# A recurrent block that starts from unscaled activations, with its norm factor applied behind its products

## What is computed

```
def rms_norm(x, g):
    y = x * rsqrt(mean(x * x, axis=-1) + 1e-6)
    return y * g

def rglru_block(h, w_in, conv_w, conv_b, w_a, b_a, w_x, b_x, lam, w_o):
    proj = h @ w_in                                   # 256 x 2048
    gate = gelu(proj[..., :1024])
    xc = causal_depthwise_conv(proj[..., 1024:], conv_w, conv_b)     # 4 taps
    r = sigmoid(per-block(xc @ w_a) + b_a)            # 16 blocks of 64 x 64
    i = sigmoid(per-block(xc @ w_x) + b_x)
    log_a = -8 * r * softplus(-lam)
    a, mult = exp(log_a), sqrt(-expm1(2 * log_a))
    hs = scan over tokens of  h = a * h + mult * i * xc
    return (hs * gate) @ w_o

x = x + rglru_block(rms_norm(x, norm_mix[1]), ...)
x = x + squared_relu_mlp(rms_norm(x, norm_mlp[1]), ...)
```

## Time and profile before

| | us |
|---|---|
| median of 3 runs (lowest, highest) | 1701.01 (1700.12, 1701.41) |
| the profiled execution, its own time | 1701.29 |
| its span | 1699.4 |
| busy over the span: PE / DVE / ACT / POOL | 1414.4 / 1087.3 / 557.2 / 530.9 |
| granted clock of PE over the span | 0.926 |

### The profile page before, as it was taken

One profiled execution on the slowest core, in us unless ns is written; L12 is line 12 of the kernel. 1 busy time (PEld: TensorE's weight loads), 2 busy tenths in 40 slices (PEclk: granted clock), 3 DMA queues, 4 the chain that ended last, 5 costly groups with the idle time before them and its releaser, 6 DMA issues.

```text
span 1699.4 us, 25116 instructions
## 1 busy us (share of the span) xinstructions
PE 1414.4 (83%) x9312; PEld 1069.9 (63%) x9312; DVE 1087.3 (64%) x2131; ACT 557.2 (33%) x1037; POOL 530.9 (31%) x620
## 2 busy tenths in 40 slices
PE   8999999986999999999988937677777648676766
PEld 7889999976999999878888823232222213222222
DVE  5556774487677456987765975757576557457435
ACT  5554653347565343432151122111121211112111
POOL 8100000010000000000000575666666666666664
PEclk9999999998999999999999968988898879888888
DMA  7444655534465453322243897999999999999997
GB/s 232 133 133 125 189 184 170 191 113 130 143 189 182 151 191 105 113 64 77 76 155 118 328 405 296 380 359 370 370 340 359 364 364 377 371 369 359 357 377 293
DMA packets 206242, 407.91 MB, mean 240 GB/s; under 512 B 10626, under 2 KB 136876, under 8 KB 206140
## 3 DMA queue, kind: packets, MB, share of 16 engines
q0 software_dynamic: 74096, 269.52, 41.2%
q1 hardware_dynamic: 131884, 136.54, 25.2%
q10 hardware_dynamic: 160, 0.53, 0.1%
HBM read 405.49 MB, written 1.05 MB: 239 GB/s over the span
## 4 chain that ended last, share of the span: by engine, by line
PE 51%; issue 14%; another core or an unknown queue 12%; DVE 11%; POOL 7%; ACT 4%; DMA 1%; POOLq 0%; DVEq 0%; SPq 0%; ACTq 0%
PE banks L2114 12%; PE banks L2116 11%; PE banks L2115 11%; PE banks L2545 3%; PE banks L2304 3%; PE banks L2580 3%; POOL arena L872 2%; POOL wring L872 2%; DVE arena L1969 2%; PE banks L2401 1%; DVE h_raw L1604 1%; PE banks L2099 1%; POOL h_raw L872 1%; ACT arena L1302 1%
## 5 line engine op out<-in xcount | busy, mean ns | idle before, releaser
L1359 DVE TENSOR_TENSOR w_a_low<-wring,w_a_high 128x1024 fp32r<-128x1024 f32 x192 | 235.0, 1226 | 128.1 <-ACT w_a_high L913 126.2
L872 POOL DMA_INDIRECT arena<-in_expert_u_dram,eidx x99 | 92.9, 939 | 656.3 <-DVEq L1949 597.3
L913 ACT ACTIVATE w_a_high<-wring 128x1024 fp32r<-128x1024 f32 x192 | 201.6, 1052 | 147.2 <-PE banks L2116 145.3
L2114 PE MATMUL banks<-h_high,w_a_high 128*128 128x256 f32 (+1 forms) x832 | 238.0, 286 | 7.9 <-DVE h_low L1367 7.3
L1302 ACT ACTIVATE arena<-ident,arena 128x128 f32<-128x128 f32 x238 | 83.9, 395 | 478.9 <-remote 249.6
L2116 PE MATMUL banks<-h_high,w_a_low 128*128 128x256 f32 (+1 forms) x832 | 235.1, 283 | 0.0
L2115 PE MATMUL banks<-h_low,w_a_high 128*128 128x256 f32 (+1 forms) x832 | 235.1, 283 | 0.0
L2580 PE MATMUL banks<-arena 128*128 128x512 f32 x340 | 169.3, 645 | 74.2 <-ACT arena L1302 40.0
L2580 PE MATMUL banks<-wring,arena 128*128 128x512 f32 x308 | 159.5, 662 | 54.5 <-issue 22.0
L2580 PEld LDWEIGHTS banks<-arena 128*128 128x128 f32 x340 | 67.1, 205 | 176.4 <-issue 128.7
L2114 PEld LDWEIGHTS banks<-h_high,w_a_high 128*128 128x128 f32 x832 | 157.8, 190 | 9.7 <-issue 7.6
(11 more groups left out here) (413 smaller groups left out, 2767.9 us busy)
## 6 DMA issues: line engine op xcount, KB each, us to landing
wring<-in_mlp_w_dram SPq DMA_DIRECT2D x64, 1024.0 KB, 5.3
wring<-in_w_in_dram SPq DMA_DIRECT2D x19, 1024.0 KB, 5.4
wring<-in_sb_w_qkv_dram SPq DMA_DIRECT2D x12, 1024.0 KB, 5.1
wring<-in_rg_w_in_dram SPq DMA_DIRECT2D x8, 1024.0 KB, 5.9
wring<-in_w_q_dram SPq DMA_DIRECT2D x8, 1024.0 KB, 5.2
wring<-in_sb_w_o_dram SPq DMA_DIRECT2D x4, 1024.0 KB, 6.3
wring<-in_rg_w_o_dram SPq DMA_DIRECT2D x4, 1024.0 KB, 5.4
wring<-in_w_o_dram SPq DMA_DIRECT2D x4, 1024.0 KB, 7.7
```

The source lines that it names most:

```text
L872: g.indirect_dma_start(out=grow(j), out_offset=None, in_=(expert_u, expert_v)[which][0], in_offset=bass.IndirectOffsetOnAxis(ap=eidx[:, tt ...
L913: a.activation(unit(n, 0), raw_unit(n), ACT.Copy).then_inc(w_high, 1)
L1359: v.tensor_tensor(unit(n, 1), raw_unit(n), unit(n, 0).bitcast(F32), ALU.subtract).then_inc(w_split, 1)
L2114: mm(dst, left[0], right[0], start=first, stop=False)
```

## The change

- `last_input` now serves both layers: in `mlp(0)` too, ACT writes the high part of x * gain and the square of each part of `xT` (4 parts after 18 of the down projection's weight splits, 2 near the end, the last 2 as they come), and DVE the low parts. `norm(2)` is gone from ACT and DVE.
- PE starts `rg0` at once, makes the norm's sums behind it (bank `ms2`), and transposes the keys behind `rg15`.
- ACT makes `rs` from the bank by Ln and Exp, as in the attention layer: no reciprocal on DVE, no square root.
- DVE takes all 16 groups out of their banks, times `rs`: rg0 to rg7 into `xraw` ahead of the taps (ACT's copy is gone), rg8 to rg15 into `gate` (`gate_input`) in pieces between the steps of the block's end. ACT's gelu then reads `gate`.
- ACT's tanh follows the sigmoids group by group (`decays`); its exponentials for `aS` stand behind each half's root.
- DVE copies the keys behind the splits of `m_hl` and three weight splits, ahead of the residual.

```diff
@@ -181,15 +181,16 @@
...
-            plan.add("ms2")
-            for m in range(4):
-                plan.add(f"key{m}")
             for m in range(KT + 2):
                 plan.add(f"rg{m}", m - KT if m >= KT else None)
+                if m == 0:
+                    plan.add("ms2")
                 if m >= 2:
                     plan.add(f"ri{m - 2}", BANKS + KT - 1 - m if m >= KT else None)
             for m in range(KT + 2, 2 * KT):
                 plan.add(f"rg{m}", m - KT)
+            for m in range(4):
+                plan.add(f"key{m}")
             for m in range(KT):
                 plan.add(f"rgo{m}")
...
@@ -927,28 +929,27 @@
...
-                if layer == 0:
-                    split_high(MLP_UNITS - hidden - UNITS)
-                    return
-                act.wait_ge(meta_ready, 1)
-                a.activation(h_hl[0][:, :, 0:META], meta_g[:], ACT.Copy).then_inc(meta_high, 1)
-                a.activation(sq[:, :, 0:META], xT[:, :, 0:META], ACT.Square).then_inc(meta_high, 1)
+                if layer:
+                    act.wait_ge(meta_ready, 1)
+                    a.activation(h_hl[0][:, :, 0:META], meta_g[:], ACT.Copy).then_inc(meta_high, 1)
+                    a.activation(sq[:, :, 0:META], xT[:, :, 0:META], ACT.Square).then_inc(meta_high, 1)
                 split_high(18)
                 for kt in range(4):
-                    last_input(kt)
+                    last_input(layer, kt)
...
                 split_high(3)
                 for kt in range(6, 8):
-                    last_input(kt)
-                split_high(2)
...
+                    last_input(layer, kt)
+                split_high(1 + layer)
+
+            def last_input(layer, kt):
+
+                gain = g_both if layer else par[:, KT:2 * KT]
+                act.wait_ge(x_ready, KT * (2 + 2 * layer) + kt + 1)
                 a.activation(h_hl[0][:, kt, real], xT[:, kt, real], ACT.Copy,
-                             scale=g_both[:, kt:kt + 1]).then_inc(h_high, 1)
+                             scale=gain[:, kt:kt + 1]).then_inc(h_high, 1)
                 a.activation(sq[:, kt, real], xT[:, kt, real], ACT.Square).then_inc(sq_ready, 1)
...
@@ -1038,7 +1039,10 @@
...
-            norm(2, whole=2, after=UNITS)
+            pb = wait_group(act, "ms2")
+            link(a.activation(rtmp[:, 0:SEQ], pb[:, 0:SEQ], ACT.Ln, bias=eps[:, 3:4]))
+            act.sem_inc(free("ms2"), 1)
+            a.activation(rs[:, 0:SEQ], rtmp[:, 0:SEQ], ACT.Exp, scale=-0.5).then_inc(rs_ready, 1)
...
@@ -1048,23 +1052,24 @@
...
+            def decays(m):
+
+                sigmoids(m)
+                act.wait_ge(ri_ready, m + 1)
+                a.activation(tS[:, m, :], rS[:, m, :], ACT.Tanh, scale=lamc[:, 3, m:m + 1]).then_inc(at_ready, 1)
+
             act.wait_ge(xc_ready, 1)
+            act.wait_ge(lam_ready, 2)
             for m in range(KT):
-                pb = wait_group(act, f"rg{m}")
-                a.activation(xraw[:, m, CONV - 1:], pb[:, 0:SEQ], ACT.Copy).then_inc(free(f"rg{m}"), 1)
                 split_high()
                 if m >= 3:
-                    sigmoids(m - 3)
+                    decays(m - 3)
...
-            sigmoids(KT - 3)
-            sigmoids(KT - 2)
+            decays(KT - 3)
+            decays(KT - 2)
             split_high()
-            sigmoids(KT - 1)
-            act.wait_ge(ri_ready, KT)
-            act.wait_ge(lam_ready, 2)
-            for m in range(KT):
-                a.activation(tS[:, m, :], rS[:, m, :], ACT.Tanh, scale=lamc[:, 3, m:m + 1]).then_inc(at_ready, 1)
+            decays(KT - 1)
...
@@ -1072,23 +1077,23 @@
...
-            for m in range(KT):
-                a.activation(aS[:, m, :], rS[:, m, :], ACT.Exp, scale=lamc[:, 4, m:m + 1]).then_inc(at_ready, 1)
             for m, h4 in enumerate(halves):
                 act.wait_ge(m_ready, m + 1)
                 a.activation(mS[:, h4], mS[:, h4], ACT.Exp, scale=0.5).then_inc(mroot_ready, 1)
-                split_high()
+                for k in range(h4.start, h4.stop):
+                    a.activation(aS[:, k, :], rS[:, k, :], ACT.Exp, scale=lamc[:, 4, k:k + 1]).then_inc(at_ready, 1)
+            for m in range(KT):
+                act.wait_ge(gate_in, m + 1)
+                a.activation(gate[:, m, :], gate[:, m, :], ACT.Gelu_apprx_tanh).then_inc(gelu_done, 1)
             split_high()
-            for m in range(KT):
-                pb = wait_group(act, f"rg{KT + m}")
-                a.activation(gate[:, m, :], pb[:, 0:SEQ], ACT.Gelu_apprx_tanh).then_inc(free(f"rg{KT + m}"), 1)
             for m in range(2):
...
                 a.activation(m_hl[0][:, h4, :], gate[:, h4, :], ACT.Copy).then_inc(gate_high, 1)
+            split_high(2)
             norm(3, whole=1, units=True)
...
@@ -1485,12 +1490,12 @@
...
+                    if k == 18:
+                        last_input(layer, 0, 4)
                     if k < hidden - UNITS:
                         split_low()
-                    if layer and k == hidden - UNITS:
-                        last_input(4, 6)
+                    if k == hidden - UNITS:
+                        last_input(layer, 4, 6)
                         split_low(2)
...
@@ -1500,21 +1505,22 @@
...
-                    if layer and k >= hidden - 2:
-                        last_input(k - hidden + KT, k - hidden + KT + 1)
+                    if k >= hidden - 2:
+                        last_input(layer, k - hidden + KT, k - hidden + KT + 1)
...
-            split_low(UNITS)
+            split_low(2)
...
@@ -1522,14 +1528,21 @@
...
-            norm(2, 1)
-            for m in range(4):
...
+            dve.wait_ge(xc_ready, 1)
+            dve.wait_ge(rs_ready, RS_AT[2])
+
+            def gate_input(first, last_):
+
+                for k in range(first, last_):
+                    pb = wait_group(dve, f"rg{KT + k}")
+                    link(v.tensor_tensor(gate[:, k, :], pb[:, 0:SEQ], rs[:, 0:SEQ], ALU.mult))
+                    dve.sem_inc(free(f"rg{KT + k}"), 1)
+                    dve.sem_inc(gate_in, 1)
 
             for m in range(KT):
-                wait_out(dve, f"rg{m}")
+                pb = wait_group(dve, f"rg{m}")
+                link(v.tensor_tensor(xraw[:, m, CONV - 1:], pb[:, 0:SEQ], rs[:, 0:SEQ], ALU.mult))
+                dve.sem_inc(free(f"rg{m}"), 1)
...
@@ -1542,28 +1555,35 @@
...
+            gate_input(0, 3)
             halves = [slice(0, KT // 2), slice(KT // 2, KT)]
             for m, h4 in enumerate(halves):
                 dve.wait_ge(at_ready, KT + 2 * m + 2)
                 link(v.tensor_tensor(mS[:, h4], mS[:, h4], tS[:, h4], ALU.subtract))
                 dve.sem_inc(m_ready, 1)
+                gate_input(3 + m, 4 + m)
...
-            dve.wait_ge(at_ready, 2 * KT + 4)
...
                 link(v.tensor_tensor(iS[:, h4], iS[:, h4], mS[:, h4], ALU.mult))
+                gate_input(5 + m, 6 + 2 * m)
+                dve.wait_ge(at_ready, KT + 4 + 4 * (m + 1))
...
                 settle()
-                split_low(2 if m else 1)
             for m, h4 in enumerate(halves):
-                wait_out(dve, *[f"rg{KT + k}" for k in range(h4.start, h4.stop)])
+                dve.wait_ge(gelu_done, h4.stop)
                 v.tensor_tensor(gate[:, h4], gate[:, h4], rS[:, h4], ALU.mult).then_inc(y_ready, 1)
...
                                 ALU.subtract).then_inc(y_split, 1)
+            split_low(3)
+            for m in range(4):
+                pb = wait_group(dve, f"key{m}")
+                v.tensor_copy(keyT[:, 4 * m:4 * m + 4, :].rearrange("p a n -> p (a n)"),
+                              pb[:, :]).then_inc(free(f"key{m}"), 1)
             residual([f"rgo{m}" for m in range(KT)], mlp_norm=3)
...
@@ -2249,26 +2269,26 @@
...
-            norm(2)
+            def gate_inputs(m):
...
+
+            for m in range(2 * KT):
+                project([f"rg{m}"], "rg_in", h_real, ready=h_wait(2) if m == 0 else None, first=m)
+                if m == 0:
+                    norm(2)
+                if 2 <= m < KT + 2:
+                    gate_inputs(m - 2)
...
-            for m in range(2 * KT):
-                project([f"rg{m}"], "rg_in", h_real, ready=h_wait(2) if m == 0 else None, first=m)
-                if 2 <= m < KT + 2:
-                    gate_inputs(m - 2)
             project([f"rgo{m}" for m in range(KT)], "rg_o", m_all, ready=lambda kt: (y_split, kt // 4 + 1))
...
```

More of the change, by code:

```diff
@@ L1487, in mlp @@
                 for k in range(hidden):
-                    if layer and k == 18:
-                        last_input(0, 4)
+                    if k == 18:
+                        last_input(layer, 0, 4)
                     if k < hidden - UNITS:
                         split_low()
-                    if layer and k == hidden - UNITS:
-                        last_input(4, 6)
+                    if k == hidden - UNITS:
+                        last_input(layer, 4, 6)
                         split_low(2)
@@ L2251, in _ @@
```

(15 more changed lines are left out.)

21 lines of the change are left out of this document (9 added, 12 removed).

## The result

| | before | after |
|---|---|---|
| median of 11 runs each, same chip, us | 1701.2 | 1685.5 |
| lowest, highest | 1692.55, 1703.22 | 1678.99, 1692.2 |
| ratio, 95% interval | | 0.9913 (0.9897 to 0.9928) |
| the profiled execution, its span | 1701.29, 1699.4 | 1684.46, 1682.7 |
| busy PE / DVE / ACT / POOL | 1414.4 / 1087.3 / 557.2 / 530.9 | 1407.3 / 1087.8 / 556.7 / 531.7 |

The kernel is faster by 12 to 17.5 us (the interval of the ratio, times 1701.2). In the block itself PE's busy time hardly moved: 84.8 us of 106.5 before, from 344.40 to the last residual addition, and 84.2 of 93.2 after, so what went there is time in which PE stood. The 7 us that PE's busy time fell by over the span lie almost all behind the block, in the same 6084 instructions (997.1 us before, 990.1 after, 1000.5 in a second profile of after).

What follows compares the result with a forecast made beforehand. PE was taken as the bound, with standstills in the head and before the output projection. First output product at 410.5 instead of 426.0 takes 15.5 us off 1701.3: 1685.8, less 0.3 is 1685.5 us; range 1682.3 to 1690.

Steps and rivals of the forecast that it cites:

- Head: From down projection to norm factor: rg0 starts without waiting, sums end at 350.85 us, `rs` ready at 351.95.
- The down projection: Rival: ACT or DVE work of `last_input` delays weight splits and PE starves, up to 6.4 us, 1692; chance 0.05.
- Convolution: Loop behind the norm sums: DVE's round 3.72 us, PE's 3.70, slack shrinking from 2.2 to 2.0; PE stays the limit.
- The rival in which DVE becomes the limit: In the convolution, DVE's round is 4.2 us, not 3.72; PE loses 1.8 us, total 1689; chance 0.16.
- Bank 0: New PE wait at rg8 until ACT frees the bank after ri4's sigmoids: 1.1 us, bounds 0 to 2.
- Block weights: Loads needed by ri0 at 356.6 us, forecast to land between 352.6 and 357.7 us.
- the rival of 0 to 1.1 us: At ri0, PE waits that long for late weights, up to 1686.6 us; counted within the forecast's chance of 0.56.
- The flip to slower: At ri0, weights landing after 372.1 us cancel the gain, from 376 slower by over 0.2%; chance 0.02.
- Tail: From rg10's end at 387.3 us to first output product, 23.2 us on DVE's chain: 410.5 instead of 426.0.
- Keys: Transpositions on PE right behind rg15, taken as 1.9 us; no wait for their banks was forecast.
- Clock: PE's clock falls to 0.50 in a 6.9 us standstill before the output products, as before: nothing gained or lost.
- Behind the tail: Output projection to residual: DVE starts 2.4 us late but catches up by the eighth group; cost 0, at most 1.

Runs made afterwards that it cites:

- all three together: Changed kernel with ri4's sigmoids earlier, block weights issued before the memset, and no DVE waits for its own gate reads: median 1684.58 us, ratio 0.9903.
- weights early: Changed kernel with block weights issued ahead of GpSimd's memset, which then writes only zero blocks: first output product 0.82 us earlier, span 1690.6 us.
- weights late: Changed kernel with GpSimd's memset of the block weights' area made four times: first output product 3.0 us later, span 1697.0 us.
- Factor first: Changed kernel with norm sums first and PE waiting for the norm factor before rg0: first output product 0.64 us later, span 1687.4 us.
- old tail: Changed kernel with tanh after the last sigmoids, exponentials ahead of roots, gate inputs behind scans: first output product at 73.71 us, not 67.78; span 1692.7 us.

## Why the prediction was right, and where it wasn't

The mechanism was right: PE's wait in the head went and the tail got shorter. 1685.5 us was forecast and measured, and part of that is luck. By the marks the block gained 13.3 us, not 15.5: the first output product came 1.8 us later than forecast, and 0.4 more went behind it. The sets of runs scatter enough to cover the difference.

- **Head**: right. rg0 starts without a wait, the factor is read at 352.35, 7.39 us behind the mark; 7.4 was forecast. The down projection didn't suffer much: its end, the mark, comes 0.4 us later, which is within what the mark differs by between runs (344.1 to 345.5).
- **Convolution**: the round was mis-sized, 3.84 us and not 3.72. The own wait behind the bank read was priced at 0.46 by the row of another read the earlier trace rows; the next instruction starts 0.57 us after it here. PE stayed the limit, but only just (all three together). The rival in which DVE becomes the limit named the right place.
- **Bank 0**: right. rg8's start was forecast 32.5 us behind the mark and comes at 33.2, with the weights early at 32.4.
- **Block weights**: the rival of 0 to 1.1 us came true with 0.52 in the row and 0.82 in effect. The flip to slower was far off. The Trainium skill, SBUF — State Buffer, SBUF: two separate sides, was cited for a DMA of the GpSimd queue that starves while DVE holds the shared port. The runs don't bear it out for these loads: with the weights early they were issued from 346.6 to 348.6 us, under the two splits that DVE ran from 347.31 for 2.35 us, and still landed in 2.8 to 3.2 us.
- **Tail**: the step that failed in size. The first output product came 67.8 us behind the mark, not 66.0. Of the 1.8, 0.5 lie ahead of rg15's end (the keys start at 402.64, 57.7 behind the mark, where 57.2 was forecast): 0.8 for the block weights, less 0.3 elsewhere. The other 1.3 are the tail's, 10.1 us in place of 8.8: 0.8 are four gate banks at 0.67 in place of 0.46 (a pair alone: 1.34 for 0.95), and 0.5 is left unassigned.
- **Keys**: not foreseen. They were put right behind rg15 (1.9 us), but their banks 5, 6, 7 and 0 come free only as DVE takes the gate. It cost nothing in the end: they ran within DVE's chain.
- **Clock**: the fall was forecast for one standstill of 6.9 us; it came with the keys in the middle of it. After, the stretch with the keys and the one before the first output product:

```profile
406.00:408.00 2.00, 1.94 (x12) 1.30 (x10) 1.76 (x4) 1.61 (x3) 0.00 (x0) 0.73 0.00 0
410.00:412.00 2.00, 0.00 (x0) 0.00 (x0) 2.00 (x3) 1.64 (x2) 0.00 (x0) 0.50 0.00 0
```

- **Behind the tail**: 0 to 1 was forecast; from first output product to last residual it took 25.25 us, before 24.88. DVE came to the residual at 419.45, 2.0 us behind the 417.4 at which rgo0 should be ready (412.74 and 4.7), 2.4 were forecast, and was idle again from 429.35.

## What to carry to other kernels

Where a product is linear in a row's norm factor, take the factor out of the way of TensorE and apply it where banks are read anyway: head and loop got 9.36 us shorter here by that and the order that it allows, for sixteen reads on DVE. Eight of these lay in the tail, where DVE had no slack except while it waited for ACT, and there they cost time unless they filled such waits. A table of banks dealt in turn ties far places together: moving four harmless groups moved a wait of 1.4 us to the ninth one. When runs scatter more than an edit is worth, measure between two instructions of the trace that repeat, with a mark close ahead of the edit so that other waits stay out of the difference, and price a wait by how much earlier the next start could be, which is more than the idle time in its row.

## What the runs showed of the hardware that was not expected

- **GpSimd's memset held DVE.** With four memsets in a row, two DVE operations on 8 columns took 1.63 and 1.83 us, and in after 0.44 and 0.17. DVE in order of time, weights late:

```profile
350.06 1.63 DVE L1528 TENSOR_SCALAR lamc<-lamc 128x8 f32<-128x8 f32 x1
351.72 1.83 DVE L1529 TENSOR_SCALAR lamc<-lamc 128x8 f32<-128x8 f32 x1
```

 POOL's row beside them:

```profile
346.12 7.41 POOL L851 MEMSET arena<- 128x2048 f32 x4 [293.37 <-DVE xT L1508]
```

 At 1.85 us each the third and fourth memset end at 351.7 and 353.5, and so do the two operations. The Trainium skill, SBUF — State Buffer, SBUF: two separate sides, calls the shared port an exclusive lock, held for the whole instruction; this agrees. Not every operation was held: the two weight splits, with both inputs in SBUF, ran at 347.11 beside the same memsets in 2.35 us, as long as in after. The hold moved DVE's first bank multiply from 7.39 to 8.67 us behind the mark.
- **The same wait, another clock.** Factor first and after reach the output projection with nearly the same work behind them. Factor first, the four us before the first output product at 412.55:

```profile
408.00:410.00 2.00, 0.38 (x2) 0.00 (x0) 1.97 (x4) 0.00 (x0) 0.00 (x0) 0.77 0.00 0
410.00:412.00 2.00, 0.00 (x0) 0.00 (x0) 2.00 (x3) 1.84 (x2) 0.00 (x0) 1.00 0.00 0
```

 There the keys ran at 0.50 (from 406 to 408), and the clock was back at 1.00 from 409, with PE idle since 408.4; in after it stayed at 0.50 until behind the first output products. From first output product to last residual it took 24.71 us against 25.25. Over all runs of the changed kernel and its variants this stage took 23.3 (old tail) to 25.8 us (weights early), so some of any gain ahead of it may be given or taken there; between factor first and after it is 0.5 us. What decides the clock was not tried.
